# Key and value cache pages on 32 partitions each in a one-core hybrid decoder step

## What is computed

```python
def fox_sample(q, k, v, log_f, k_past, v_past, lf_past):
    past, t = k_past.shape[1], q.shape[1]
    lf_past = lf_past.astype(jnp.float32)
    r_past = lax.cumsum(lf_past, axis=1, reverse=True) - lf_past
    c_new = jnp.cumsum(log_f, axis=1)
    keys = jnp.concatenate([k_past, k.astype(k_past.dtype)], axis=1)
    vals = jnp.concatenate([v_past, v.astype(v_past.dtype)], axis=1)
    c_k = jnp.concatenate([-r_past, c_new], axis=1)
    return fox_attend(q, c_new, past + jnp.arange(t), keys, vals, c_k, jnp.arange(past + t))
```

## Time and profile before

| what | value |
|---|---|
| median of 3 executions | 1046.34 us |
| lowest, highest | 1034.18, 1046.88 us |
| the profiled execution's own time | 1055.26 us |
| its span, first to last instruction | 1053.7 us |
| its granted TensorE clock, mean | 0.864 of 2.4 GHz |
| PE, DVE, ACT, POOL busy | 83%, 34%, 17%, 15% of the span |
| moved by DMA | 219.02 MB, mean 208 GB/s |
| cache block in it | about 445 to 650 us of the span |

### The profile page before, as it was taken

How to read it: one execution, slowest core, us unless ns; L and a number is a source line. 1 busy time by engine, 2 the same in 40 slices (tenths; PEclk the granted TensorE clock), 3 DMA queues, 4 the chain that set the end, 5 groups by cost and what they waited for, 6 DMA issues and landing times. The chain is left out here.

```text
span 1053.7 us, 20823 instructions
## 1 busy us (share of the span) xinstructions
PE 869.9 (83%) x8785; PEld 522.9 (50%) x8785; DVE 359.3 (34%) x647; ACT 183.3 (17%) x407; POOL 154.0 (15%) x296
## 2 busy tenths in 40 slices
PE   4998999896798995779878875997568878988884
PEld 3445666565565674436656743642554234533321
DVE  2003223495225331486576610202540241021123
ACT  2003112163211000132121112001111001110102
POOL 8100200243002002103344340100000000000000
PEclk9998999898896585987796685999589989999998
DMA  8323222113121201378999997311729994599992
GB/s 333 145 80 120 93 80 80 62 67 111 27 69 42 42 16 50 123 236 277 386 386 385 384 395 279 120 40 40 305 100 422 421 421 191 239 420 421 421 412 72
DMA packets 66103, 219.02 MB, mean 208 GB/s; under 512 B 17567, under 2 KB 21962, under 8 KB 49626
## 3 DMA queue, kind: packets, MB, share of 16 engines
q1 hardware_dynamic: 55264, 186.03, 46.3%
q0 software_dynamic: 10096, 31.48, 8.1%
q10 hardware_dynamic: 650, 0.18, 0.1%
HBM read 210.96 MB, written 6.70 MB: 207 GB/s over the span
## 5 line engine op out<-in xcount | busy, mean ns | idle before, releaser
L2131 PE MATMUL bank<-arena 128*32 128x512 f32 x512 | 78.5, 634 | 20.7 <-DMA arena<-in_w_exp 19.3
L218 PE MATMUL bank<-arena 128*128 128x336 f32 x256 | 90.0, 497 | 4.3 <-PEq L107 4.3
L1714 DVE STREAM_TRANSPOSE arena<-arena 128x2048 f32<-128x2048 f32 x32 | 73.3, 2299 | 17.0 <-DMA arena<-in_ck 16.0
L1528 POOL DMA_DIRECT2D arena<-in_cv x112 | 60.3, 538 | 117.5 <-PE bank L1647 89.1
L484 PE MATMUL bank<-arena 128*128 128x336 f32 x224 | 71.1, 474 | 4.2 <-DVE arena L630 4.2
L2111 PE MATMUL bank<-arena 128*128 128x128 f32 x432 | 54.4, 289 | 17.2 <-DVEq L2296 9.6
L218 PEld LDWEIGHTS bank<-arena 128*128 128x128 f32 x256 | 50.4, 207 | 30.3 <-issue 11.2
L2111 PEld LDWEIGHTS bank<-arena 128*128 128x128 f32 x432 | 52.7, 204 | 23.9 <-DVEq L2296 9.7
L463 PE MATMUL bank<-arena 128*128 128x512 f32 (+1 forms) x144 | 62.1, 593 | 0.0
L484 PEld LDWEIGHTS bank<-arena 128*128 128x128 f32 x224 | 43.9, 200 | 27.3 <-issue 10.0
L1647 PE MATMUL bank<-arena 128*16 128x128 f32 x1024 | 36.3, 293 | 23.9 <-DMA arena<-in_cv 16.7
(11 more groups left out here) (452 smaller groups left out, 1123.0 us busy)
## 6 DMA issues: line engine op xcount, KB each, us to landing
arena<-in_w_exp SPq DMA_DIRECT2D x99, 1024.0 KB, 18.3
arena<-in_ck SPq DMA_DIRECT2D x128, 256.0 KB, 8.5
arena<-in_cv POOLq DMA_DIRECT2D x112, 256.0 KB, 7.5
arena<-in_w_gate SPq DMA_DIRECT2D x8, 1024.0 KB, 4.8
arena<-in_w_za SPq DMA_DIRECT2D x7, 1024.0 KB, 7.0
arena<-in_w_zb SPq DMA_DIRECT2D x6, 1024.0 KB, 13.7
arena<-in_cv SPq DMA_DIRECT2D x16, 256.0 KB, 3.2
arena<-in_w_proj SPq DMA_DIRECT2D x4, 1024.0 KB, 19.3
```

The lines of the kernel that those rows point to most:

```text
L218: mm = nc.tensor.matmul(bank[b][:, 0:T], w[:, k, a, :], xnT[:, k, :], start=(k == 0), stop=(k == KT - 1))
L1528: eng.dma_start(dst, src[bass.ds(page, 1)].rearrange("a p n -> (a p) n")).then_inc(sem, 16)
L1714: nc.vector.transpose(kT[b % 2][:, :, 128 * m:128 * m + 128].rearrange("p j (n k) -> p n j k", n=4), slot[m].rearrange("p (n j k) -> p n j ...
L2131: mm = nc.tensor.matmul(bank[2][j * CAP:(j + 1) * CAP, :], xg[:, q % 2, k, j * CAP:(j + 1) * CAP], wslot[s][:, (k % 4) * 512:(k % 4 + 1) * ...
```

## The change

A page is now loaded as 32 rows of 8 KB, each row four tokens. The four pages of a slot stand one above the other, page n on partitions 32n to 32n + 31. Partition 32n + p then holds tokens 4p to 4p + 3 of page n, where before partition p held token p of all four. The loads still move 256 KB each, in the same order, from the same queues and behind the same waits. The transposes, scores, probabilities and value products keep their code; what was the n-th page in a slot is now the tokens 4p + n of all four pages.

The decay sums have to come in the new order. The sums over later pages are made first: PE multiplies `tot` with `after` (8 columns), DVE copies the result behind the 128 tokens of `lfg`, as a 129th. The eight transposes take tokens 1 to 128, so that each column is the next token's value, the last one the later pages' sum. Sixteen products with the shifted triangle `tri4` then add up within a page and put the tokens in the slot's order. `later` and the products with `ones` are gone. PE now spreads the queries first, then waits for `tot`, then for the copy, then transposes. DVE waits for PE's product before it goes on to `turn_keys`. POOL makes two more masks in `rwkv_post`.

```diff
+        def page_load(eng, tile, n, src, page, sem):
+            eng.dma_start(tile[32 * n:32 * n + 32, :], src[bass.ds(page, 1)].rearrange("a (p j) n -> (a p) (j n)", j=4))\
+                .then_inc(sem, 16)
+
         def load_pages(sp, s, pages):
             src = A["ck"] if s < 4 else A["cv"]
             for n in range(4):
-                sp.dma_start(slot[s][:, n * BW:(n + 1) * BW],
-                             src[bass.ds(pages[n], 1)].rearrange("a p n -> (a p) n")).then_inc(full[s], 16)
+                page_load(sp, slot[s], n, src, pages[n], full[s])
...
-        later = pre(DB * NPAGES, NH)
-        lfg = pre(PAGE * NH)
+        lfg = pre((PAGE + 1) * NH)
+        tri4 = pre(4, P + 96)
...
-                ch(nc.gpsimd.memset(tri_key, 1.0))
-                ch(nc.gpsimd.affine_select(out=tri_key, in_=tri_key, compare_op=ALU.is_gt, fill=0.0, base=0,
+                ch(nc.gpsimd.memset(tri4, 0.0))
+                tv = tri4[:, :, 96:P]
+                ch(nc.gpsimd.memset(tv, 1.0))
+                ch(nc.gpsimd.affine_select(out=tv, in_=tv, compare_op=ALU.is_ge, fill=0.0, base=0,
+                                           pattern=[[-1, 4], [-4, 32]], channel_multiplier=1))
+                ch(nc.gpsimd.memset(tri_page, 1.0))
+                ch(nc.gpsimd.affine_select(out=tri_page, in_=tri_page, compare_op=ALU.is_gt, fill=0.0, base=0,
                                            pattern=[[-1, P]], channel_multiplier=1))
...
-        def page_load(eng, dst, src, page, sem):
-            eng.dma_start(dst, src[bass.ds(page, 1)].rearrange("a p n -> (a p) n")).then_inc(sem, 16)
...
-                            page_load(sp, page_part(slot[m], n), A["ck"], pages[n], full[m])
+                            page_load(sp, slot[m], n, A["ck"], pages[n], full[m])
...
-                            page_load(nc.gpsimd, page_part(slot[4 + m], n), A["cv"], pages[n], vpool[m])
+                            page_load(nc.gpsimd, slot[4 + m], n, A["cv"], pages[n], vpool[m])
...
             def _(pe):
-                lv = lfg.rearrange("p (k h) -> p k h", h=NH)
-                for h in range(NH):
-                    mm = nc.tensor.transpose(bank[h // 4][:, (h % 4) * P:(h % 4 + 1) * P], lv[:, :, h], ident)
-                    if h % 4 == 3:
-                        mm.then_inc(S("lfT_ps"), 1)
                 for s in range(4):
...
                     mm.then_inc(S("qs_ps"), 1)
+                pe.wait_ge(S("tot_sb"), 1)
+                nc.tensor.matmul(bank[2][:, 0:NH], after, tot, start=True, stop=True).then_inc(S("later_ps"), 1)
+                pe.wait_ge(S("later_sb"), 1)
+                lv = lfg.rearrange("p (k h) -> p k h", h=NH)
+                for h in range(NH):
+                    mm = nc.tensor.transpose(bank[h // 4][:, (h % 4) * P:(h % 4 + 1) * P], lv[:, 1:PAGE + 1, h], ident)
+                    if h % 4 == 3:
+                        mm.then_inc(S("lfT_ps"), 1)
                 pe.wait_ge(S("lfT_sb"), 2)
-                pe.wait_ge(S("later_ready"), 1)
-                for q in range(2):
-                    n = slice(64 * q, 64 * q + 64)
-                    nc.tensor.matmul(bank[2 + q][:, :], tri_key, lfT[:, :, n].rearrange("p h n -> p n h"),
-                                     start=True, stop=False)
-                    nc.tensor.matmul(bank[2 + q][:, :], ones, later[:, n, :].rearrange("p n h -> p (n h)"),
-                                     start=False, stop=True).then_inc(S("rsuf_ps"), 1)
+                for j in range(4):
+                    for n in range(4):
+                        mm = nc.tensor.matmul(bank[2 + j // 2][:, (j % 2) * 256:(j % 2 + 1) * 256],
+                                              tri4[:, j, 96 - 32 * n:96 - 32 * n + P],
+                                              lfT.rearrange("p h (a n) -> p a h n", n=4)[:, :, :, n],
+                                              start=(n == 0), stop=(n == 3))
+                    if j % 2:
+                        mm.then_inc(S("rsuf_ps"), 1)
...
             def _(act):
-                for q in range(2):
-                    act.wait_ge(S("lfT_ps"), q + 1)
...
+                rv = rsuf[:, 0:DB * NPAGES * NH].rearrange("p (a j h) -> p j a h", j=4, h=NH)
                 for q in range(2):
                     act.wait_ge(S("rsuf_ps"), q + 1)
-                    nc.scalar.activation(rsuf[:, 512 * q:512 * q + 512], bank[2 + q][:, :], ACT.Copy)\
+                    nc.scalar.activation(rv[:, 2 * q:2 * q + 2],
+                                         bank[2 + q][:, :].rearrange("p (j a h) -> p j a h", j=2, h=NH), ACT.Copy)\
                         .then_inc(S("rsuf_sb"), 1)
...
-                ch(nc.vector.tensor_reduce(tot, lfg.rearrange("p (k h) -> p h k", h=NH), AX.X, add))
-                ch(nc.vector.tensor_tensor(later, bc(after, 2, NH), bc(tot, 1, DB * NPAGES), mult))
-                dve.sem_inc(S("later_ready"), 1)
+                nc.vector.tensor_reduce(tot, lfg[:, 0:PAGE * NH].rearrange("p (k h) -> p h k", h=NH), AX.X, add)\
+                    .then_inc(S("tot_sb"), 1)
+                dve.wait_ge(S("later_ps"), 1)
+                nc.vector.tensor_copy(lfg[:, PAGE * NH:], bank[2][:, 0:NH]).then_inc(S("later_sb"), 1)
                 for m in range(4):
                     turn_keys(0, m)
```

More of the change, by code:

```diff
@@ L1404, in build @@
         lfT = pre(NH, DB * NPAGES)
-        later = pre(DB * NPAGES, NH)
-        lfg = pre(PAGE * NH)
+        lfg = pre((PAGE + 1) * NH)
+        tri4 = pre(4, P + 96)
         osb = sp5(P)
-        tri_key = osb
+        tri_page = osb
         tot = small[:, 208:208 + NH]
@@ L1437, in _ @@
                 pool.sem_inc(S("bonus_b"), 1)
-                nc.gpsimd.indirect_dma_start(lfg, None, A["clf"], bass.IndirectOffsetOnAxis(ap=pt_col[:, 0:1], axis=0))\
+                nc.gpsimd.indirect_dma_start(lfg[:, 0:PAGE * NH], None, A["clf"], bass.IndirectOffsetOnAxis(ap=pt_col[:, 0:1], axis=0))\
                     .then_inc(S("lfg_in"), 16)
-                ch(nc.gpsimd.memset(tri_key, 1.0))
-                ch(nc.gpsimd.affine_select(out=tri_key, in_=tri_key, compare_op=ALU.is_gt, fill=0.0, base=0,
+                ch(nc.gpsimd.memset(tri4, 0.0))
[5 more added lines that the diff above has]
+                ch(nc.gpsimd.affine_select(out=tri_page, in_=tri_page, compare_op=ALU.is_gt, fill=0.0, base=0,
                                            pattern=[[-1, P]], channel_multiplier=1))
-                ch(nc.gpsimd.affine_select(out=after, in_=tri_key, compare_op=ALU.is_ge, fill=0.0, base=NPAGES - 1,
+                ch(nc.gpsimd.affine_select(out=after, in_=tri_page, compare_op=ALU.is_ge, fill=0.0, base=NPAGES - 1,
                                            pattern=[[NPAGES, DB], [0, NPAGES]], channel_multiplier=-1))
@@ L1674, in _ @@
             def _(act):
-                for q in range(2):
-                    act.wait_ge(S("lfT_ps"), q + 1)
-                    nc.scalar.activation(lfT[:, 4 * q:4 * q + 4, :], bank[q][:, :].rearrange("p (h n) -> p h n", h=4),
-                                         ACT.Copy).then_inc(S("lfT_sb"), 1)
                 act.wait_ge(S("qs_zero"), 1)
@@ L1685, in _ @@
                 for q in range(2):
+                    act.wait_ge(S("lfT_ps"), q + 1)
+                    nc.scalar.activation(lfT[:, 4 * q:4 * q + 4, :], bank[q][:, :].rearrange("p (h n) -> p h n", h=4),
+                                         ACT.Copy).then_inc(S("lfT_sb"), 1)
+                rv = rsuf[:, 0:DB * NPAGES * NH].rearrange("p (a j h) -> p j a h", j=4, h=NH)
+                for q in range(2):
                     act.wait_ge(S("rsuf_ps"), q + 1)
-                    nc.scalar.activation(rsuf[:, 512 * q:512 * q + 512], bank[2 + q][:, :], ACT.Copy)\
+                    nc.scalar.activation(rv[:, 2 * q:2 * q + 2],
+                                         bank[2 + q][:, :].rearrange("p (j a h) -> p j a h", j=2, h=NH), ACT.Copy)\
                         .then_inc(S("rsuf_sb"), 1)
```

## The result

The changed kernel takes 1157.18 us (median of 4, 1152.67 to 1164.69) against 1046.61 for the kernel before: a ratio of 1.109, 95% interval 1.098 to 1.120. It is slower by 10 to 11%; the forecast was 9% (1141 us, of a range of 1078 to 1190). The profiled execution of the kernel before was a slow one, 8.7 us above this median, so a few microseconds between stretches of the two traces prove nothing by themselves.

A forecast was written before the change was run, and what follows sets the result against it. The cache block was taken as bound by its DMA transfers. Pages +98, slack -6 and decay sums +3 summed to +95 us on the median of 1046.3, giving 1141 us, range 1078 to 1190.

The forecast's parts named there:

- The bound and the mechanism: Cache block: ends when its bytes have landed; engines with rows in neighbouring partitions seem to share a way into SBUF.
- The 91 ns row of `in_xs`: Merge's prompt loads: with only 64 partitions left, DMA engines take 91 ns per KB, 127 GB/s at share 0.72.
- Rival 1: Cache block pages: no sharing, rows of 8 KB run like weights, -11 us for pages, 1038 us; chance 0.12.
- rival 2: Cache block pages: half shared, 52 ns per KB, 315 GB/s, +34 us for pages, 1078 us; chance 0.10.
- rival 3: Cache block pages: worse than two to a way, 180 GB/s, +174 us for pages, 1217 us; chance 0.06.
- Rival 4: Cache block: only the decay chain counts, pages as before, +4 us, 1050 us; chance 0.03.
- The pages: Cache block: page loads at 70 ns per KB, 235 GB/s, take 250 us instead of 152, +98 us.
- the tenth off two to a way: Cache block pages: 70 ns per KB taken instead of 77, since keys and values from two queues lose some sharing.
- The slack: First 40 us of the cache block, DMA share 0.81: slower key pages fill it, 6 of 7.6 us come off.
- The decay sums: Cache block start: scores 4 us later but covered, transposes and transfer stream 2 us later; +3 us, bounds 0 to 5.
- Signs named ahead: Cache block: share near 1.0, rate falling to about 235 GB/s, last key issue about 675; expert block keeps 421 GB/s.
- Pages of sequence 0: Issued in earlier blocks: each slot's 1 MB takes 4.5 instead of 2.7 us; costs nothing, at most 3 us.

The follow-up runs named there:

- e3: Changed kernel with each page's 32 rows of 8 KB on every fourth partition, decay sums to match; ratio 1.015 to the kernel before.
- e6: Kernel before with a page as 64 rows of 4 KB on 64 partitions in one piece; 1135.3 us, one execution.
- e7: Kernel before with a page as 64 rows of 4 KB on every second partition; 1038.1 us, one execution.
- e1: Kernel before with only the change's page loads, decay sums as before; ratio 1.096 to the kernel before, 1147 us.
- e11: Repeat of e1, the kernel before with only the change's page loads; ratio 1.094 to the kernel before.
- e10: The changed kernel measured again, nothing altered; ratio 1.101 to the kernel before.
- the three pairs above: Cache block, new decay chain against old: 9.7 us longer with pages of before, 10.1 to 13.6 in one piece, 8.2 on every fourth partition.
- e4: Changed kernel with POOL loading the four pages of a value slot in the order 2, 3, 0, 1; ratio 1.095 to the kernel before.
- e8: Changed kernel with its sixteen decay products cut to the triangle's 32 nonzero columns, each to its own 32 partitions; ratio 1.098, 1147 us.

## Why the prediction was right

*The bound and the mechanism.* Both stood. The 91 ns row of `in_xs` against the 38 ns row of the weights was the main argument, and e3, e6 and e7 show what it meant: the place of the partitions. That it is neighbouring partitions that share is not shown, as e6 says. Rival 1 (four pages on four sets share out the ways) is refuted by the changed kernel itself, rival 2 (52 ns) and rival 3 (91 ns) by its 72 ns. Rival 4 is out too: the rate didn't stay at 385. The argument against rival 3, four rows on a way against two, was no argument: with two rows to an engine and two engines to a way, as the forecast has it, 32 partitions put four rows on a way as well.

*The pages.* Forecast 70 ns a KB, 235 GB/s, +98 us, and 6 off for the slack, +92. In the stretch of 180 us it is 71 ns and 230 GB/s; 58.7 MB at that are 255 us, +103. The blocks of e1 and e11, which have the pages and not the chain, are 93.4 and 93.8 us longer than the one before. So this part came out within a few microseconds. That is partly luck: the tenth off two to a way had no row behind it, and its reason, engines that drift apart, stays unshown.

*The slack.* Forecast: 6 of 7.6 us come off. From the first key reload on, the share of the first 40 us rises from 0.81 to 0.98 in e1 and e11, 6.8 us, but only to 0.92 in e10, 4.4 us: the late chain holds the rest open. The forecast also took 32 key pages, 8.4 MB, for all that moves there; the stretch before moved 258 x 40 us, 10.3 MB, with 39 key and 6 value pages issued in it. That would only have filled it sooner.

*The decay sums.* This step was mis-sized, and is most of what the forecast lacks: "sixteen products of 256 columns at half of 1.98 / 2 each, 8 us". The row of L1588 says x2 and 1.98 us, and I read two products where the code issues one; an f32 product shows as two records. Half of 1.98, sixteen times, is 15.8 us, and 14.5 came. So the scores are 10.8 us later and not 4. DVE's first transposes are 3.0 us later and not 2. And "the scores' 4 us are covered while the pages are late" failed: the chain costs 8 to 14 us of the block in the three pairs above (7.6 by the medians), where I took 3, of bounds 0 to 5.

Together: the block grew by 107.0 us (103.9 in e10) where the forecast has 95. Of these 9 to 12 us the chain makes 7 to 11, the pages with their slack 1 to 2. The median of the first measurement is 16 us above the forecast, and by e10's ratio it would be 11; what the block doesn't explain of it lies behind the block or in the noise.

*Signs named ahead.* The share stayed at 1.0 while the rate fell, and the expert block kept 421 GB/s. The last key issue came at 655.5, not 675; a larger part than I thought came behind it, +30.5 us. PE's clock fell to 0.65 in the block, but not to its lower level throughout. Pages of sequence 0 cost nothing that the rows show.

*Not foreseen:* 5.8 us behind the block, 408.7 for 402.9. SP's issue of 32 expert weights, which spans the routing, took 99.2 us for 93.7, also in e10 and e11 (99.0, 100.3). But it is no cost of pages in one piece as such: e4 and e6 have these too, and 402.9 and 402.8 us behind the block, and in e4 that issue took 92.7. What sets it stays open.

## What to carry to other kernels

A transfer's rate hangs on which partitions it touches, not only on how long its rows are. Spread a tile that has fewer than 128 rows over the whole width instead of putting it in one block: 32 rows on every fourth partition and 64 on every second are what was tried here. 32 rows on every second partition would lie within 64 in one piece, and nothing here says that this helps. Read the DMA share together with the rate: where the share stays at 1.0 and the rate falls, the engines work longer for each KB (here by the place of the partitions, and a little by the length of the rows); a share that falls is a late issue or a late wait. Before counting instructions off a grouped row, see how many records one of them makes. And don't write a delay off as covered before looking at the share in the very stretch in which it falls.

## What the runs showed of the hardware

- 32 partitions in one piece, f32 rows of 8 KB, in the changed kernel: 216 to 253 GB/s in windows of 30 us, with the engines busy throughout. Every fourth of 128: 391 to 396. 64 in one piece, rows of 4 KB: 240; every second of 128: 382.
- The rate of transfers in one piece isn't steady within one block at an unchanged share. In windows of 30 us from 510 on it is 216, 216, 228, 231 and 253 GB/s in the changed kernel, and 226, 256, 267, 242 and 234 in e4.
- Four products of 32 columns each, to four sets of 32 output partitions, ran side by side: a record lasts 0.62 us in e8 as in the changed kernel, but the 32 records of the sixteen products of 256 columns take 3.8 us together instead of 14.5.

The first agrees with the Trainium skill ("SBUF — State Buffer", section on the DMA port swizzle), which has 8 of 16 ports for 32 and for 64 partitions in one piece and an asymptote of 218 GB/s: the first 60 us of the full block, 216, are at it. The later windows, up to 253, lie above it, and there the measurement decides. Its section on two DMAs for both halves gives +6% for them; no run here sets up just that, and e4's 244 GB/s over 510 to 690 us is not told from the 242 and 243 of e11 and e8.
